# Two transformer blocks on one core: weight splits ordered around the attention's links, and cross-attention laid beside its own projection

## The reference, cut to what matters

```
proj = h @ w_in[l]            # xr, gr, q, k, v, g_rnn, g_attn
y_rnn  = rglru(conv(xr)) * gelu(gr)
y_attn = softmax(band(q k^T / 8), sink) v        # 16 query heads, 2 key heads, window 128
merged = sigmoid(g_rnn) * (y_rnn @ w_br_rnn) + sigmoid(g_attn) * (y_attn @ w_br_attn)
h = LN(ALPHA * h + merged @ w_out)
q = h @ cq_w ; k, v = split(mem @ ckv_w)         # cross-attention, 4 heads of 256
h = LN(ALPHA * h + softmax(q k^T / 16) v @ co_w)
h = LN(ALPHA * h + (silu(h @ wi_gate) * (h @ wi_up)) @ ffn_wo)
```

```
for e in range(16):
    out += gate[:, e] * ((silu(t @ w1[e]) * (t @ w3[e])) @ w2[e])
```

## Time and profile before

| what | value |
|---|---|
| median of 3 runs | 1680.62 us (1676.35 to 1683.83) |
| the profiled execution's own time | 1681.34 us |
| its span | 1679.4 us |
| PE (matmul) busy | 1596.6 us, 95% |
| DVE busy | 1151.0 us, 69% |
| ACT busy | 903.9 us, 54% |
| mean DMA rate | 202 GB/s |

### The profile page before, as it was taken

The page is one execution under the profiler, slowest core; times in us unless marked ns, Lnnn a source line. Parts: engine busy times, 40 slices in busy tenths (PEclk is TensorE's granted clock), DMA queues, the critical chain, the costliest instruction groups (busy, mean ns, idle before and its releaser), DMA issues.

```text
span 1679.4 us, 20455 instructions
## 1 busy us (share of the span) xinstructions
PE 1596.6 (95%) x8036; PEld 1303.4 (78%) x8036; DVE 1151.0 (69%) x1617; ACT 903.9 (54%) x1377; POOL 79.7 (5%) x75
## 2 busy tenths in 40 slices
PE   7999999989999999989999899999989969999997
PEld 7987788776888789878878667888767758777786
DVE  7457655657545584667566478866664669999997
ACT  5466443435444364764434254544353448888885
POOL 0010000001000000100000000000200000000005
PEclk9999999999999999999999999999999879999999
DMA  7445234535654454542356278874440318999995
GB/s 286 177 153 198 89 112 158 194 126 211 242 198 177 149 202 175 204 172 86 116 200 226 75 259 296 315 257 175 150 169 26 119 63 302 364 374 369 370 371 177
DMA packets 52202, 339.35 MB, mean 202 GB/s; under 512 B 7835, under 2 KB 8477, under 8 KB 13316
## 3 DMA queue, kind: packets, MB, share of 16 engines
q1 hardware_dynamic: 48932, 331.79, 53.7%
q0 software_dynamic: 3168, 6.20, 1.0%
HBM read 332.82 MB, written 10.49 MB: 204 GB/s over the span
## 4 chain that ended last, share of the span: by engine, by line
PE 70%; DVE 15%; ACT 8%; DMA 3%; issue 3%; POOL 1%; ACTq 0%; DVEq 0%; SPq 0%
PE bank L199 66%; DVE wls L211 6%; PE bank L203 4%; ACT whs L207 3%; DMA raw<-in_ws_dram 3%; ACT arena L208 1%; DVE arena L211 1%; DVE sm L222 1%; ACT P1h L1847 1%; DVE h L211 1%; DVE arena L219 1%; POOL sm L231 1%; DVE arena L844 1%; ACT arena L207 1%; DVE arena L215 1%
## 5 line engine op out<-in xcount | busy, mean ns | idle before, releaser
L211 DVE TENSOR_TENSOR wls<-raw,whs 128x1024 fp32r<-128x1024 f32 x442 | 523.5, 1227 | 243.4 <-ACT whs L207 242.8
L207 ACT ACTIVATE whs<-raw 128x1024 fp32r<-128x1024 f32 x442 | 443.2, 1051 | 276.1 <-PE bank L199 193.3
L199 PE MATMUL bank<-whs,P1h 128*128 128x512 f32 (+1 forms) x732 | 291.2, 398 | 5.2 <-DVE P1l L1849 2.0
L199 PE MATMUL bank<-whs,P1l 128*128 128x512 f32 (+1 forms) x732 | 285.5, 390 | 0.0
L199 PE MATMUL bank<-wls,P1h 128*128 128x512 f32 (+1 forms) x732 | 285.1, 390 | 0.0
L199 PE MATMUL bank<-whs,P0h 128*128 128x512 f32 (+1 forms) x640 | 257.6, 402 | 6.3 <-DVE P0l L211 2.5
L199 PE MATMUL bank<-whs,P0l 128*128 128x512 f32 (+1 forms) x640 | 250.2, 391 | 0.0
L199 PE MATMUL bank<-wls,P0h 128*128 128x512 f32 (+1 forms) x640 | 250.1, 391 | 0.0
L199 PEld LDWEIGHTS bank<-whs,P1h 128*128 128x128 f32 x732 | 138.4, 189 | 36.2 <-DVE P1l L211 3.6
L199 PEld LDWEIGHTS bank<-whs,P1l 128*128 128x128 f32 x732 | 138.3, 189 | 29.2
L199 PEld LDWEIGHTS bank<-wls,P1h 128*128 128x128 f32 x732 | 138.4, 189 | 26.9
(11 more groups left out here) (267 smaller groups left out, 2497.1 us busy)
## 6 DMA issues: line engine op xcount, KB each, us to landing
raw<-in_ws_dram SPq DMA_DIRECT2D x264, 1024.0 KB, 4.9
landing<-in_ws_dram SPq DMA_DIRECT2D x38, 1024.0 KB, 7.1
lnb<-in_ln_g_dram SPq DMA_DIRECT2D x6, 512.0 KB, 5.8
lnb<-in_ln_b_dram SPq DMA_DIRECT2D x6, 512.0 KB, 6.5
ydram<-arena POOLq DMA_DIRECT2D x4, 512.0 KB, 11.8
mid<-in_bias_dram SPq DMA_DIRECT2D x1, 2048.0 KB, 7.6
h<-in_x_dram SPq DMA_DIRECT2D x2, 512.0 KB, 4.0
lnb<-in_mem_dram SPq DMA_DIRECT2D x1, 1024.0 KB, 13.1
```

Source lines behind the costliest of these rows:

```text
L199: return PE.put(lambda e: e.matmul(out, lhsT, rhs, start=start, stop=stop, skip_group_check=skip), w, inc)
L207: return AC.put(lambda e: e.activation(out, in_, func, bias=bias, scale=scale), w)
L211: return VE.put(lambda e: e.tensor_tensor(out, a, b, op), w)
```

## The change

It has five parts.

1. **Order of splits.** `split_half` puts the high part on ACT and defines the low part as a function. In a new mode `two`, set with `slow` from `w_br_rnn` to the end of `ckv_w` in each mixer, the low part is kept back: a tick first puts one high part, then the link of `side`, then the low part. `release` then pumps nothing. `half_of` lets the matmuls on the first half of a unit wait for the first half's token alone, in every large product of the kernel.
2. **Mixer attention.** The key copies move ahead of the recurrence into the free `lnb`; q and k are turned in three smaller links; `turn` is three and `weigh` five links behind `scores` (17 links); the row sums are finished in `scores` and `turn`; the result is turned in two links with four banks. `C["yT"]` keeps both tokens.
3. **Cross-attention.** The second `cq_w` product runs beside `attend`, and `weigh` of heads 2 and 3 beside the first `co_w` product.
4. **Router.** The low parts of the first token tile are put around the norm of the second, a weight split is moved behind, `Pall` is built right behind `v_place` and ahead of the branch, and `gather` does all 16 matmuls of tile 0 first.
5. **Start.** The first half of `h` is loaded ahead of the identity and the condition.

```diff
@@ split_half
-            tok = split([x[:, c] for x in slots[j]], raw_of(n)[:, c], here(n), free=free)
-            state["half"] = 1 - f
-            if f:
-                state["split"] += 1
-                split_tok[n] = [split_tok[n], tok]
-                raw_free[n] = tok
-                emit_dma()
+            (hi, lo), src = [x[:, c] for x in slots[j]], raw_of(n)[:, c]
+            a = act(hi, src, ACT.Copy, here(n), free)
+            def low():
+                tok = tt(lo, src, f32(hi), ALU.subtract, a)
+                state["half"] = 1 - f
+                if f:
+                    state["split"] += 1
+                    split_tok[n] = [[split_tok[n]], [tok]]
+                    raw_free[n] = tok
+                    emit_dma()
...
+            if state["two"]:
+                lows.append(low)
             else:
-                split_tok[n] = tok
+                low()
+        def half_of(tok, kk, per):
+            return tok[0] if isinstance(tok, list) and 2 * kk < per else tok
         def tick():
             state["n"] += 1
+            if state["two"] and not lows:
+                split_half()
             if state["n"] % state["pace"] == 0 and side and next(side[0], "end") == "end":
                 side.pop(0)
-            if state["slow"]:
+            if state["slow"] and not state["two"] or lows:
                 feed(1)
@@ start
+        c_h = [load(h[:, 0, :], xr[:, 0, :], s="d_h0")]
         c_ident = load(ident[:, :], ins["ident"], s="d_ident")
         c_cond = load(sm[:, 640:656], ins["cond"], s="d_cond")
-        c_h = [load(h[:, t, :], xr[:, t, :], s=f"d_h{t}") for t in range(2)]
+        c_h.append(load(h[:, 1, :], xr[:, 1, :], s="d_h1"))
@@ gemm_tm, and alike in gemm_fm, up_chunk, down_chunk, up, down
-                            part(w, slice(None), kk), first, closes and kk == per - 1, tok,
+                            part(w, slice(None), kk), first, closes and kk == per - 1, half_of(tok, kk, per),
@@ mixer
+            kd = lnb[:, 0, 0:512].rearrange("p (a b) -> p a b", a=2)
+            for t in range(2):
+                for g in range(2):
+                    kready = vcopy(kd[:, t, 128 * g:128 * g + 128]..., C["rot"], L["lnb"])
-                    C["yT"] = split(part(P1, slice(None), s_), xc[:, s_, :], v, free=L["P1"])
+                    C["yT"].append([split(part(P1, slice(None), s_), xc[:, s_, :], v, free=L["P1"])])
+                turn_q(0, 0)
...
+                yield
+                turn_q(0, 1)
+                turn_q(1, 0)
+                yield
+                turn_q(1, 1)
+                yield
-                for i in range(n + 4):
-                    if i >= 4:
-                        weigh(i - 4)
-                    if 2 <= i < n + 2:
-                        turn(i - 2)
+                for i in range(n + 5):
+                    if i >= 5:
+                        weigh(i - 5)
+                    if 3 <= i < n + 3:
+                        turn(i - 3)
                     if i < n:
                         scores(i)
                     yield
+                for t in range(2):
+                    C["yfm"].append(to_fm(qkv[:, t, 0:1024], ..., tb=((7, 5), (6, 4))[t])[0])
+                    yield
+            state["slow"] = state["two"] = True
-            src = [(P1, t, [C["yT"]]) for t in range(2)]
+            src = [(P1, t, C["yT"]) for t in range(2)]
...
             finish_side()
+            state["slow"] = state["two"] = False
@@ cross
-            for c in range(2):
-                gemm_fm("cq_w", P0, N["t"], (2 * c, 2 * c + 1), q_evac(c), by_unit=True)
+                for t in range(2):
+                    scores(t, 0)
+                    yield
+                yield
                 turn(0)
                 turn(1)
+                for t in range(2):
+                    scores(t, 1)
+                for hd in range(2):
+                    weigh(hd)
+                    oT[0].append(X[("o", hd)])
+                turn(2)
+                turn(3)
                 yield
+                for hd in range(2, 4):
+                    weigh(hd)
+                    oT[1].append(X[("o", hd)])
+                yield
+            gemm_fm("cq_w", P0, N["t"], (0, 1), q_evac(0), by_unit=True)
+            finish_side()
             at = attend()
-            next(at)
             side.append(at)
-            finish_side()
+            gemm_fm("cq_w", P0, N["t"], (2, 3), q_evac(1), by_unit=True)
             gemm_tm("co_w", src, lambda i: i, res_evac(rs, 0))
+            finish_side()
@@ merge_evac of w_out_2
+                    if t:
+                        fT[0][2](0)
                     xn_[t] = ts(xs[:, t, :], h[:, t, :], smv(o + 5, 1), None, ALU.mult, None, g, Q["ph"])
+                    if t:
+                        fT[0][2](1)
+                        state["slow"], state["hold"] = False, True
...
-        feed(2)
+        feed(3)
@@ places
-        v_off = vcopy(offi[:, :], begins, d_)
         v_place = tt(second, second, first, ALU.subtract, a_, d_)
+        for t in range(2):
+            p_ = ts(Pall[:, t, :], count, first[:, t:t + 1], None, ALU.is_equal, ...)
+            p_at.append(stt(Pall[:, t, :], count, second[:, t:t + 1], ...))
         v_slot = ts(slot, slot, -1.0, None, ALU.add, None, v, v_place)
+        v_off = vcopy(offi[:, :], begins, v_slot)
@@ gather
-                    for i in range(4):
-                        t, p = i // 2, i % 2
-                        m = mm(banks[k][:, :], rows[p][:, t, ...], Pall[:, t, :], i == 0, i == 3, p_, ...)
+                    for p in range(2):
+                        mm(banks[k][:, :], rows[p][:, 0, ...], Pall[:, 0, :], p == 0, False, p_at[0], ...)
+                for k in range(8):
+                    for p in range(2):
+                        m = mm(banks[k][:, :], rows[p][:, 1, ...], Pall[:, 1, :], False, p == 1, p_at[1], ...)
```

More of the change, by code:

```diff
@@ L294, in build @@
         split_tok = {}
-        state = {"start": None, "half": 0, "slow": False, "dma": 0, "split": 0, "take": 0, "pace": 1, "n": 0, "hold": False, "loose": False, "between": False}
+        state = {"start": None, "half": 0, "slow": False, "dma": 0, "split": 0, "take": 0, "pace": 1, "n": 0, "hold": False, "loose": False, "between": False, "two": False}
         def here(n):
@@ new lines, in attention, with turn_q @@
+                tok = []
+                def turn_q(t, g):
+                    b = 7 if g else 6
+                    for j in range(4):
+                        m = tr(banks[b][:, j * 128:(j + 1) * 128], qkv[:, t, (4 * g + j) * 128:(4 * g + j + 1) * 128],
+                               C["rot"], bankfree[b], inc=(j == 3))
+                    a = act(qT[:, 4 * g:4 * g + 4, t * 128:(t + 1) * 128],
+                            banks[b][:, :].rearrange("p (a b) -> p a b", a=4), ACT.Copy, m, e0)
+                    bankfree[b] = [a]
+                    tok.append(a)
@@ new lines, in attention @@
+                turn_q(0, 0)
+                for g in range(2):
+                    for t in range(2):
+                        m = tr(banks[5][:, (2 * g + t) * 128:(2 * g + t + 1) * 128], kd[:, t, g * 128:(g + 1) * 128],
+                               kready, bankfree[5], inc=(g + t == 2))
+                L["lnb"] = m
+                a = vcopy(kT, banks[5][:, :].rearrange("p (a b) -> p a b", a=2), m, e0)
+                bankfree[5] = [a]
+                tok.append(a)
+                yield
@@ L1066, in q_evac @@
                 return evac
-            for c in range(2):
-                gemm_fm("cq_w", P0, N["t"], (2 * c, 2 * c + 1), q_evac(c), by_unit=True)
-            xfree = PE.last()
             den, mx, nm = smv(256, 8), smv(264, 8), smv(272, 8)
@@ L1653, in build @@
         yfree = PE.last()
-        for n in range(2):
-            fT[0][2](n)
         fT = [fT[0][0], f_fm(1, False)[0]]
+        state["slow"], state["hold"] = True, False
         count = arr(5632, 512)
@@ L1773, in build @@
         v_place = tt(second, second, first, ALU.subtract, a_, d_)
+        p_at = []
+        for t in range(2):
+            p_ = ts(Pall[:, t, :], count, first[:, t:t + 1], None, ALU.is_equal, None, n_, v_place, Q["ph"])
+            p_at.append(stt(Pall[:, t, :], count, second[:, t:t + 1], f32(Pall[:, t, :]), ALU.is_equal, ALU.add, p_))
         v_slot = ts(slot, slot, -1.0, None, ALU.add, None, v, v_place)
+        v_off = vcopy(offi[:, :], begins, v_slot)
         def finish(done, T={}):
@@ L1810, in gather @@
                 z = [GP.put(lambda e, x=x: e.memset(x[:, :, 512:640], 0.0), [start]) for x in xall]
-                for t in range(2):
-                    p_ = ts(Pall[:, t, :], count, first[:, t:t + 1], None, ALU.is_equal, None, n_, v_place, start)
-                    p_ = stt(Pall[:, t, :], count, second[:, t:t + 1], f32(Pall[:, t, :]), ALU.is_equal, ALU.add, p_)
                 T["gate"] = gates_()
```

90 lines of the change are left out of this document (39 added, 51 removed).

## The result

The changed kernel takes 1633.56 us (median of 4, 1632.06 to 1635.28) against 1678.81 for the one before (median of 4 by then): a ratio of 0.9727, 95% interval 0.970 to 0.9754. A second set of five runs gave 0.9732 (0.9713 to 0.9751). The forecast was 1647 with a range of 1636 to 1662.

What follows compares the result with a forecast made beforehand. The prediction took PE, busy 95% of the span and holding 70% of the chain, as the bound. Gains of 20.4 + 8.0 + 0.9 + 2.2 + 2.3 = 33.8 us from 1681.3 gave 1647.5, forecast 1647, range 1636 to 1662.

Steps and rivals of the forecast that it cites:

- the mixer term: Mixer attention of both layers: waits and half-clock stretches removed, less new waits, gain 20.4 us, bounds 12 and 22.4.
- `half_of` in the experts: Expert loop: PE waits for no split there, so nothing is gained.
- the sum: Whole kernel: gains of 33.8 us taken from the profiled 1681.3 give 1647.5, with the lower median 1647.
- the same bounds of 44.9: Whole kernel: upper bounds 22.4 + 14 + 1.5 + 3.8 + 3.2 together, 44.9 us below 1681, setting the low end 1636.
- Mixer attention, removed: Both mixers: six PE waits per layer (8.68 and 8.64 us) and three half-clock stretches (5.1) go, gross 22.4.
- Mixer attention, added: Both mixers: more links fit into 5.40 us each; new waits cost 2.0 us, bounds 0 and 5.6 in each layer.
- Cross-attention: Cross-attention, both layers: 15.0 us of waits and dips removed, 7.0 left, gain 8.0, bounds 2 and 14.
- The dip: Cross-attention: the half-clock loss of 1.7 us stays with a 4 in 10 chance, allowed 0.7 in each layer.
- a rule that short idle times make the clock fall: Cross-attention, from the Trainium skill: remaining stalls keep a dip in each layer, 2.0 us more, near 1649.
- `half_of`: Around `w_in` (1.0 us per layer) and 1200 to 1250 (1.8): PE starts on first halves, gain 2.2, bounds 0 and 3.8.
- Start: First product: starts earlier but runs at half clock, gain 0.9 us, bounds 0.4 and 1.5.
- Router: PE's 5.70 us wait ahead of the gather: some 3.2 earlier, gain 2.3, bounds 1.0 and 3.2; low parts 0 net.

Runs made afterwards that it cites:

- the old attention: The changed kernel with the whole mixer attention of before (key copies, two-link turns, 16 + 3 links, late row sums, one-link result, pumped splits): 1660.29 us.
- the old gather: The changed kernel with `Pall` built behind the branch and bank after bank for both tiles, as before; router low parts stay as changed: 1637.25 us.
- the old lows: The changed kernel with the low parts of the router's first tile behind `w_out_2` and the weight split where it was, `Pall` still early: 1634.67 us.
- the old order of splits: The changed kernel with its new attention links, but splits pumped at each release as before, neither `slow` nor `two` set: 1649.94 us.
- both parts ahead: The changed kernel with one half for each tick, but its high and low part both ahead of the link: 1658.33 us.
- no `half_of`: The changed kernel with every matmul waiting for both halves of its unit, as before: 1639.27 us.
- the kernel without pumping: The changed kernel with `slow` on during the second `cq_w` product, so a release pumps no splits and each tick puts one half behind the link: 1629.88 us.

## Why the prediction was wrong in size

The causes named were right for the mixers, the start and the router. The step that failed is the size of the mixer term: 22.4 us removed less 2.0 added, 20.4 in all, where the two pairs of profiles show 23.8 and 24.3, and 25.4 when the old attention is put back. A second term failed outright: `half_of` in the experts was put at nothing and is worth 1.5 to 1.7. Beside these the sum stood on one profile, at 1681.3, while the kernel's median of ten is 1678.6. From there the same bounds of 44.9 would have ended at 1633.7 and not at 1636, so that the time lies below the range by this more than by the terms.

Point by point, in its own order.

*Mixer attention, removed: right in cause, too small.* All six waits and the three half-clock stretches went, as said. The gross was put at 22.4 us and the experiment with the old attention gave 25.4. The idle times in the rows begin at the modelled end of a matmul. Counted from start to start, the 2.82 is 2.99 and the 1.53 is 1.70; twelve such waits make some 2 us. The half-clock stretches were read from one profile too: it has 10.2 us of them in the mixers, the second of before and that with the old attention 13.7, which is 1.7 us of loss more.

*Mixer attention, added: near in size, by an argument that doesn't hold.* 2.0 us were allowed for new waits (up to 5.6), argued from DVE's 4.3 of 5.40 us in a link. There is one new wait in each layer, 0.7 us from start to start, 1.4 together. But the 5.40 are from a link beside `ckv_w`. Beside `w_br_rnn` the links are 4.5 us apart and DVE has no room to speak of (15.53 of 16.10 us). What decided was whether a piece of work stands in the ring of DVE and ACT and makes DVE wait. With the low part in the ring PE waits 4.4 us at once, with it outside nothing, at the same amount of work. The prediction named the low part's place and costed it only as a queue position of 1.23 us. (It counts 23 links; its terms, 3, 17 and 2, make 22.)

*Cross-attention: right in size, wrong in what makes the wait.* Forecast 8.0, measured 8.9 and 8.7. The wait ahead of the third turn, in place of those of the earlier trace rows, was put at 2.0 and is 1.61. It was given to the softmax, with only two `weigh` over it, and the splits that `release` pumps were given 0.4 in another place. Without pumping 0.20 of the wait is left, so the pumped splits made 1.4 of it and the softmax does nearly fit: that the 2.0 came out is luck. The dip was given 4 in 10 for each layer and came in one of two, in both profiles:

```profile
344.70:348.11 3.41, 3.23 (x8) 2.58 (x9) 0.63 (x2) 0.00 (x0) 0.00 (x0) 0.50 0.07 26
```

That is the level of 1.2 GHz, right behind waits of 1.61 and 0.41 us; layer 2 has the same two waits and no such stretch. Of a rule that short idle times make the clock fall (the Trainium skill, TensorE: Matmul & The Clock Gate, A second HAM failure mode: psum-queue depth-cycling) these runs show that they can, not that they do each time. Eight profiles have the waits of 1.61 and 0.41 us in layer 1: four have the stretch behind them (the changed kernel twice, the old gather, the old lows) and four have none (the old attention, the old order of splits, both parts ahead, no `half_of`). In layer 2 one of the eight has it, that without `half_of`. With the wait at 0.2, in the kernel without pumping, neither layer has one, which by this count may be chance. The prediction's own remark, that only waits of 2.82 and 3.04 had dips behind them, leaves out the one at 249.4 to 252.8, behind waits of 0.99 and 0.82.

*`half_of`: in good part the wrong place.* The 1.0 us of each `w_in` came (0.75 each) and was given back 40 us later. Of the 1.8 us at 1200 to 1250 nothing can be told: the second block gained 0.6 and 1.9 in the two pairs, with the clock in both. It pays at the start (up to 0.8), in the second feed-forward (0.9 to 2.3, in one profile of it undone) and in the experts, 0.13 to 0.17 at each of eleven places, where the text said that PE waits for no split: the waits there are of PE's weight loads and under 0.5 us each, and were read as none. Together the stages explain 2.6 to 4.8 of the 4 to 6 that the median says.

*Start: right, with luck in it* (0.9; 1.2 and 0.9). PE started the first product 1.97 us earlier and kept 1.19; in the second pair 1.51 and 0.92. The slow matmuls, 0.21 us apart, ended at 17.2 and 18.5 us in the two profiles of before, and at 16.8 and 18.3 in the two of after, that is 0.2 to 0.4 us earlier for a start 1.5 to 2.0 earlier. But in the twelve profiles of the changed kernel and its variants they end anywhere from 15.4 to 18.3, so these pairs don't settle whether the slow beginning lasts for an amount of time, and the stage's gain can be off by 1 us either way.

*Router: 2.3 forecast, 2.6 measured* for the gather, and 0 for the low parts, as said. The four parts of `Pall` take 2.51 us by their own rows (1370.98 to 1373.49) and not 2.3, and the wait fell by 2.48; of the "some 3.2 earlier" the rest did not come.

*Left out: waits and half-clock stretches outside the parts.* The profile of before was one draw. It lost 3.3 us more in the second layer's feed-forward than the next did, and it had 1.6 us of half-clock gather, which both profiles of before have; the prediction counted neither. Its median, 1680.62 of three, was itself 2 above that of ten (1678.6).

So of the 12.8 us by which the first pair of profiles beats the sum, mixers and `w_in` make 2.8, the feed-forward 4.8 (3.3 of them luck), router and gather 1.5, the experts 1.5, cross-attention 0.9, the second block 0.6, the rest small. The low end of the range was the sum of the parts' upper bounds, 44.9, and these were bounds only for what was counted: feed-forward and experts stood in it with 0.

What stays open: what `half_of` does to the transfers of the second feed-forward, and what places the stretches at 0.50 between 1150 and 1290. They add up to 23.9 us in both kernels' first profiles, 17.1 in that with the old lows (which gained 3.7 us there) and 27.3 in that without `half_of`; one kernel's times spread by 6 us or more, and of what the profiles show these stretches and the second feed-forward are the largest parts.

## What to carry to other kernels

Where two in-order engines feed each other inside a repeated step, draw the ring of what waits for what, and keep every instruction that is not part of it behind the last one that is: here one subtraction of 1.2 us, moved from ahead of a step to behind it, was worth over 20 us of 1650. Ahead of the step it made DVE idle for 2.69 us in a round; behind it DVE was nearly full and still kept up. When the cause of a wait is "two splits were in the queue first", look for the same cause in the next stage too; the same cure took 1.4 us of wait out of each cross-attention. And profile the kernel before twice: a stage's wait that is gone in the second is nobody's gain, and one that is there again, like the late transfer here, is not luck.

## What the runs showed of the hardware

- A half-clock stretch costs about half of its length where PE works through it. The changed kernel lost 3.2 us across its 6.83 us stretch at 1218.5 to the run with the old lows, which had none there, and 1.5 us across the 3.41 us at 344.7 to the run with the old attention.
- The same waits (1.61, then 0.41 us) brought a stretch at 0.50 in four of eight profiles in layer 1 and in one of eight in layer 2. Two executions of the changed kernel agreed in this.
- The first product's slow matmuls (0.21 us for 256 columns instead of 0.12) ended between 15.4 and 18.3 us in twelve executions, in which the first of them started between 11.6 and 13.5.
